# A hybrid decoder layer on one core: joint last tiles in three stages, and a final normalization that goes by thirds of the rows

## The reference

```python
h = rmsnorm(x, g_mix); z = h @ w_in            # 6656 columns: qa ka va ga (1024 each), qb 1024, kb 256, vb 256, gb 1024
oa = combine(dilated attention of 16 heads, windows/steps (128,1) (512,4) (2048,16))
ob = sliding window attention, 16 query heads, 4 key heads, 128 keys back, with sinks
h  = x + concat(oa * silu(ga), ob * silu(gb)) @ w_out
y  = h + (p @ w_ple) * sigmoid(rmsnorm(h, g_ple) @ w_pg)
return rmsnorm(y, g_final), and the new keys and values
```

## Time and profile before

| | |
|---|---|
| time, median of 3 runs | 2685.92 us (2680.72 to 2686.15) |
| the profiled execution's own time | 2688.74 us |
| its span, first to last instruction | 2686.9 us |
| TensorE busy | 2468.8 us (92%) |
| VectorE, ScalarE, POOL busy | 861.3, 610.3, 621.5 us |
| mean granted TensorE clock | 0.958 |
| mean DMA rate | 107 GB/s |

### The profile page before, as it was taken

How to read it: one execution, slowest core, us unless ns; L and a number is a source line. 1 busy time by engine, 2 the same in 40 slices (tenths; PEclk the granted TensorE clock), 3 DMA queues, 4 the chain that set the end, 5 groups by cost and what they waited for, 6 DMA issues and landing times.

```text
span 2686.9 us, 40432 instructions
## 1 busy us (share of the span) xinstructions
PE 2468.8 (92%) x16617; PEld 2298.9 (86%) x16617; DVE 861.3 (32%) x2136; ACT 610.3 (23%) x1458; POOL 621.5 (23%) x653
## 2 busy tenths in 40 slices
PE   4999999999999999999899887899999969999970
PEld 3998888888888898888788887799999859999970
DVE  7022332332332304445544223231101163323224
ACT  5022222222222213335454000120000131101013
POOL 2222222222222232222111321234333201111110
PEclk7999999999999999999999998899999979999995
DMA  4132222232322234434443442443323253232326
GB/s 170 57 117 93 87 91 91 91 97 85 96 90 83 70 99 133 136 112 131 143 121 116 130 142 76 135 145 95 89 75 90 78 184 96 73 96 74 94 70 235
DMA packets 301962, 287.95 MB, mean 107 GB/s; under 512 B 20865, under 2 KB 267449, under 8 KB 298425
## 3 DMA queue, kind: packets, MB, share of 16 engines
q1 hardware_dynamic: 278898, 241.11, 29.8%
q10 hardware_dynamic: 17856, 27.34, 3.0%
q0 software_dynamic: 5024, 16.92, 1.7%
HBM read 215.48 MB, written 69.81 MB: 106 GB/s over the span
## 4 chain that ended last, share of the span: by engine, by line
PE 83%; DVE 7%; DMA 6%; ACT 2%; issue 1%; POOL 1%; SPq 1%; POOLq 0%; DVEq 0%; ACTq 0%
PE psum L813 18%; PE psum L815 17%; PE psum L814 17%; PE psum L886 5%; PE psum L888 5%; PE psum L887 5%; PE psum L618 3%; PE psum L634 3%; PE psum L646 3%; DMA s_ring<-in_cache_a_v 1%; PE psum L837 1%; DMA out<-f_out 1%; PE psum L674 1%; DMA s_ring<-in_cache_a_k 1%; PE psum L689 1%
## 5 line engine op out<-in xcount | busy, mean ns | idle before, releaser
L813 PE MATMUL psum<-act_hi,w_hi 128*128 128x344 f32 x3264 | 1078.9, 331 | 14.1 <-DVE act_lo L1364 13.1
L815 PE MATMUL psum<-act_hi,w_lo 128*128 128x344 f32 x3264 | 1051.9, 322 | 0.0
L814 PE MATMUL psum<-act_lo,w_hi 128*128 128x344 f32 x3264 | 1051.5, 322 | 0.0
L813 PEld LDWEIGHTS psum<-act_hi,w_hi 128*128 128x128 f32 x3264 | 623.6, 191 | 25.7 <-issue 20.1
L814 PEld LDWEIGHTS psum<-act_lo,w_hi 128*128 128x128 f32 x3264 | 622.7, 191 | 0.0
L815 PEld LDWEIGHTS psum<-act_hi,w_lo 128*128 128x128 f32 x3264 | 622.1, 191 | 0.0
L575 POOL CAST w_hi<-w_raw 128x512 fp32r<-128x512 f32 x272 | 182.4, 671 | 1547.9 <-PE psum L815 1406.6
L577 POOL TENSOR_TENSOR w_lo<-w_raw,w_hi 128x512 fp32r<-128x512 f32 x272 | 366.5, 1348 | 21.8
L1162 DVE COPY prob_t<-psum 128x512 f32<-128x512 f32 (+2 forms) x96 | 53.5, 558 | 470.0 <-PE psum L646 470.0
L584 POOL DMA_DIRECT2D y_scratch<-y_nat x48 | 36.7, 764 | 425.1 <-ACT y_nat L1092 415.5
L886 PE MATMUL psum<-act_hi,u_even 128*128 128x344 f32 x384 | 125.5, 327 | 9.4 <-DVE u_even L1387 8.3
(11 more groups left out here) (198 smaller groups left out, 2742.1 us busy)
## 6 DMA issues: line engine op xcount, KB each, us to landing
w_raw<-in_w_in SPq DMA_DIRECT2D x208, 256.0 KB, 3.0
w_raw<-in_w_out SPq DMA_DIRECT2D x64, 256.0 KB, 2.8
u_raw<-in_w_pg SPq DMA_DIRECT2D x16, 1024.0 KB, 6.3
z_scratch<-stage ACTq DMA_DIRECT2D x72, 172.0 KB, 1.8
h_scratch<-h_row ACTq DMA_DIRECT2D x16, 516.0 KB, 3.3
h_stage<-h_scratch SPq DMA_DIRECT2D x16, 516.0 KB, 4.7
h_in<-h_scratch SPq DMA_DIRECT2D x48, 172.0 KB, 2.6
x_in<-in_x_prompt SPq DMA_DIRECT2D x8, 1024.0 KB, 5.1
```

Of the source, the lines that this page charges most:

```text
L813: pe.matmul(psum[:, bank, 0:T3], w_hi[:, slot, x, :], act_hi[:, k, rows], start=(k == 0), stop=False, skip_group_check=True)
L814: pe.matmul(psum[:, bank, 0:T3], w_hi[:, slot, x, :], act_lo[:, k, rows], start=False, stop=False, skip_group_check=True)
L815: return pe.matmul(psum[:, bank, 0:T3], w_lo[:, slot, x, :], act_hi[:, k, rows], start=False, stop=stop, skip_group_check=True)
```

## The change

The input projection's last two tiles (52 - 2 = 50 on, `ZPAIR` = unit 150) are made together, k outermost, with six banks; so are the last two output tiles (`HPAIR` = 14). While they are made, y tiles 0 to 13 (h tiles 0 to 13) are loaded back and split in the places of `act_hi` and `act_lo` that the joint tiles have used up (`x_used`, `yk_used`). The y tiles of the pair itself stay in SBUF (`y_last`). All 16 output tiles have k outermost. p is turned beside output tiles 1 to 9. Squares of h are summed in thirds. Gate tile 0 has k outermost, and the three mean matmuls stand behind its k = 11 and k = 14.

Gate weights go through the same groups, raw slots and ring as the others (4 groups of 4 k tiles and one of 2 per tile), loaded by SP and split by POOL; those of the last tile have their own space (`last_hi`, `last_lo`). Gate tiles 14 and 15 go third by third of the rows (`GATES`). The squares of y are summed from PSUM by ScalarE, piece by piece, and ScalarE issues the stores to `y_scratch`. When a third of both last tiles is done, its rows are loaded back into the parts of `act_hi` and `act_lo` that it frees (`f_rows`), the two last column tiles are put beside them from PSUM, and the rows are scaled by VectorE (or, for pieces 2, 4 and 5, by POOL) and stored.

In `events()` the sample sequences stand 88 places apart instead of 96, with other offsets, and mixer B's part is moved ahead, with its eight score transposes in one place (`sb` 1). g_ple is loaded at the start.

```diff
+GATES = [(n, t) for n in range(KT - 2) for t in range(3)] + [(n, t) for t in range(3) for n in (KT - 2, KT - 1)]
+GSPLIT = 3 * (KT - 2)
+ROW_PIECES = [(T3 * t + c0, n) for t in range(3) for c0, n in PIECES[t]]
...
+        first = 1448 + 88 * b
+        for i, at in enumerate((0, 1, 16, 22, 34, 72)):
             put(first + at, "sa_load", b, i)
-        for t, at in enumerate((8, 13, 24)):
+        for t, at in enumerate((8, 13, 26)):
             put(first + at, "sk", b, t)
...
+        for step, at in ((1, 42), (2, 58), (3, 70), (4, 83), (5, 87)):
             put(first + at, "sa", b, step)
-    put(2226, "sb_rows")
-    put(2240, "sb", 0)
+    put(2160, "sb_rows")
+    put(2174, "sb", 0)
     for b in range(NB):
-        put(2250 + 14 * b, "sb_seq", b)
-    put(2370, "sb", 1)
-    put(2400, "sb", 2)
-    put(2420, "sb", 3)
-    put(2440, "sb", 4)
+        put(2184 + 14 * b, "sb_seq", b)
+    put(2330, "sb", 1)
+    put(2350, "sb", 2)
+    put(2366, "sb", 3)
+    put(2382, "sb", 4)
...
+        last_hi, = at(B0 + 3072, ("last_hi", [P, KT + 2, P], F32R))
+        last_lo, = at(B0 + 16512, ("last_lo", [P, KT + 2, P], F32R))
+        squares, f_rms = at(B0 + 34400, ("squares", [P, 9, KT], F32), ("f_rms", [P, 5, 3], F32))
...
+        f_rows = [place(1, 0), place(1, P), place(0, 0), place(1, T3), place(1, T3 + P), place(0, T3), place(0, T3 + P), place(1, 0), place(1, P)]
+        gf_row = place(0, P)
...
+            sp.dma_start(gcol[:], a["g_ple"].rearrange("a (k p) -> p (a k)", p=P), allow_slow_non_contiguous=True).then_inc(sem("consts"), 16)
...
+            sp.wait_ge(sem("sb_done"), 1)
+            sp.wait_ge(sem("y_gated"), ZPAIR - GATE0)
+            for j in range(6):
+                i, t = divmod(ZPAIR - GATE0 + j, 3)
+                w = T3 if t < 2 else S - 2 * T3
+                sp.dma_start(o_last[:, j, 0:w], o_dram[i, :, T3 * t:T3 * t + w]).then_inc(sem("o_last_loaded"), 16)
+            for slot, count in stored(ZPAIR - 1):
                 sp.wait_ge(sem(f"stored{slot}"), 16 * count)
...
+            first = GROUP["in", NZ - 2, 0]
+            for k in range(HPAIR):
+                if k >= 3:
+                    sp.wait_ge(sem("y_split"), k - 2)
+                sp.dma_start(y_in[:, k % 3, :], yt_dram[k]).then_inc(sem(f"y_loaded{k % 3}"), 16)
+                if k % WG == 1 and k > WG:
+                    weights(first + 2 * (k // WG) + 5)
+                    weights(first + 2 * (k // WG) + 6)
             load_x_cols(0)
...
+            weights(first + 13)
+            weights(first + 14)
...
+            for n in range(KT - 2):
+                first = GROUP["gate", n, 0]
+                for t in range(2):
+                    load_h_in(3 * n + t)
                 if n:
...
-            sp.wait_ge(sem("u_produced"), 3 * KT)
+                    load_h_in(3 * n + 2)
+                for part in range(5 if n < KT - 3 else 10):
+                    weights(first + part + 7)
+                if n == 0:
+                    load_h_in(2)
+            def load_f(i):
+                r0, n = ROW_PIECES[i]
+                cols = (KT - 2) * P
+                sp.dma_start(f_rows[i][0:n, 0:KT - 2, :], y_dram[r0:r0 + n, 0:cols].rearrange("p (k c) -> p k c", c=P)).then_inc(sem(f"f_loaded{i}"), 16)
+            def store_f(i, count):
+                r0, n = ROW_PIECES[i]
+                sp.wait_ge(sem("f_scaled"), count)
+                m = min(n, S - r0)
+                sp.dma_start(yp[r0:r0 + m, :].rearrange("p (k c) -> p k c", c=P), f_rows[i][0:m]).then_inc(sem("out_stored0"), 16)
+                if m < n:
+                    sp.dma_start(ys.rearrange("p (k c) -> p k c", c=P), f_rows[i][m:n]).then_inc(sem("out_stored0"), 16)
+            for u in range(3):
+                load_h_in(GSPLIT + u)
             for par in range(2):
...
+                sp.wait_ge(sem(f"y_stored{par}"), 32 * (GSPLIT // 2))
+            sp.wait_ge(sem("u_produced"), GSPLIT + 2)
+            for i in range(3):
+                load_f(i)
+            sp.dma_start(gf_row, bcast_rows(a["g_final"].rearrange("(a d) -> a d", a=1), P).rearrange("p (k c) -> p k c", c=P)).then_inc(sem("gf_loaded"), 16)
+            load_h_in(GSPLIT + 3)
+            store_f(0, 1)
+            store_f(1, 2)
+            sp.wait_ge(sem("u_produced"), GSPLIT + 4)
+            for i in range(3, 7):
+                load_f(i)
+            sp.wait_ge(sem("out_stored0"), 32)
+            load_f(7)
+            load_f(8)
+            load_h_in(GSPLIT + 4)
+            load_h_in(GSPLIT + 5)
+            store_f(3, 3)
+            for i in range(6, 9):
+                store_f(i, i - 2)
+            sp.wait_ge(sem("out_stored0"), 16 * 7)
+            sp.wait_ge(sem("out_stored1"), 16 * 3)
...
+                last = what in ("gate", "ple") and i == KT - 1
                 pool.wait_ge(sem(f"w_loaded{g % 2}"), 16 * (g // 2 + 1))
...
+                if last:
+                    k += KT if what == "ple" else 0
+                    hi, lo = last_hi[:, k:k + n], last_lo[:, k:k + n]
+                    if k == 0:
+                        pool.wait_ge(sem("h_split"), KT)
+                        pool.wait_ge(sem("h_summed"), 3 * KT)
+                        for par in range(2):
...
+            pool.wait_ge(sem("gf_loaded"), 16)
+            for done, i in enumerate((2, 4, 5)):
+                r0, n = ROW_PIECES[i]
+                pool.wait_ge(sem(f"f_loaded{i}"), 16)
+                pool.wait_ge(sem("f_inverted"), i // 3 + 1)
+                pool.tensor_tensor(f_rows[i][0:n], f_rows[i][0:n], gf_row[0:n], ALU.mult).then_inc(sem("f_weighed"), 1)
+                pool.wait_ge(sem("f_weighed"), 2 * done + 1)
+                pool.tensor_scalar(f_rows[i][0:n], f_rows[i][0:n], f_rms[0:n, 1 + i // 3, i % 3:i % 3 + 1], None, ALU.mult).then_inc(sem("f_weighed"), 1)
+                pool.wait_ge(sem("f_weighed"), 2 * done + 2)
+                pool.dma_start(yp[r0:r0 + n, :].rearrange("p (k c) -> p k c", c=P), f_rows[i][0:n]).then_inc(sem("out_stored1"), 16)
...
+                elif e[0] == "sb" and e[1] == 1:
+                    pe.wait_ge(sem("bnew_scored"), 1)
+                    pe.wait_ge(sem("sa_ended"), 2 * NB)
+                    pe.transpose(psum[0:HEADS, 5, 0:NB], bnew[:], ident[0:NB, 0:NB]).then_inc(sem("bnew_rowed"), 1)
+                    pe.wait_ge(sem("sb_copied"), 3)
+                    pe.wait_ge(sem("sb_scored"), NB)
+                    for b in range(NB):
+                        mm = pe.transpose(psum[0:HEADS, 2 + b // 4, P * (b % 4):P * (b % 4 + 1)], bsc[:, b, :], ident[:])
+                    mm.then_inc(sem("sb_rowed"), 1)
...
+            pe.wait_ge(sem("bank_free"), ZPAIR)
+            pe.wait_ge(sem("sb_done"), 1)
+            for k in range(KT):
+                for i in range(2):
+                    group_wait("in", NZ - 2 + i, k)
+                    for t in range(3):
+                        mm = three(3 * i + t, "in", NZ - 2 + i, k, t, k == KT - 1)
+                        if k == KT - 1:
+                            mm.then_inc(sem("produced"), 1)
+                    if k < KT - 1 and i == 1:
+                        mm.then_inc(sem("x_used"), 1)
+                    elif k < KT - 1 and k % WG == WG - 1:
+                        mm.then_inc(sem("w_used"), 1)
...
+            pe.wait_ge(sem("h_bank_free"), 3 * HPAIR)
             for k in range(KT):
...
+                for i in range(2):
+                    group_wait("out", HPAIR + i, k)
+                    for t in range(3):
+                        mm = three(h_banks[i][t], "out", HPAIR + i, k, t, False)
+                    if i == 1:
+                        mm.then_inc(sem("yk_used"), 1)
+                    elif k % WG == WG - 1:
+                        mm.then_inc(sem("w_used"), 1)
+            residual(HPAIR)
+            residual(HPAIR + 1)
...
+            pe.wait_ge(sem("p_lo"), len(ROW_TILES))
+            for k in range(KT):
+                group_wait("gate", 0, k)
+                pe.wait_ge(sem("h_split"), k + 1)
                 for t in range(3):
...
+                    if k == 0 and t == 2:
+                        pe.wait_ge(sem("h_bank_free"), 3 * HPAIR + 1)
+                    mm = three(4 + t, "gate", 0, k, t, k == KT - 1)
+                if k % WG == WG - 1:
+                    mm.then_inc(sem("w_used"), 1)
+                if k == 11:
+                    pe.wait_ge(sem("h_summed"), 3 * KT)
+                    pe.wait_ge(sem("h_bank_free"), 3 * KT)
+                    mean_square(0)
+                    mean_square(1)
+                elif k == 14:
+                    pe.wait_ge(sem("h_eps"), 1)
+                    mean_square(2)
+            for t in range(3):
+                embedding(t)
+            for u in range(3, 3 * KT):
+                n, t = GATES[u]
+                pe.wait_ge(sem("p_read"), u - 2)
+                for k in range(KT):
+                    if t == 0:
+                        group_wait("gate", n, k)
```

(33 more changed lines are left out.)

551 lines of the change are left out of this document (288 added, 263 removed).

## The result

| | before | changed | ratio, 95% interval |
|---|---|---|---|
| median | 2683.3 us (4 runs) | 2596.4 us (2594.6 to 2596.9, 4 runs) | 0.9676 [0.9659, 0.9692] |
| span of the profiled execution | 2686.9 | 2595.1 | |
| mean granted TensorE clock | 0.958 | 0.972 | |
| TensorE, VectorE, ScalarE, POOL busy | 2468.8, 861.3, 610.3, 621.5 | 2451.2, 831.8, 635.0, 711.8 | |

The account below looks back on a forecast made before the run. TensorE is busy throughout the long product stretches; only its stops and the low clock after them can be won. Terms +1.5 - 65 - 14 + 3 - 34 - 43 = -151.5 from 2688.7, less 2.8, gave 2535 us; range 2505 to 2585.

Parts of the forecast that it names:

- The mechanisms of the joint tiles: Last two input and last two output tiles: products hide loading and splitting of earlier tiles; -14 and -34 us.
- A single stop: Sign in the gate: TensorE stops once, about 5 us, after the first gate tile, ended by t_gate or p_read on VectorE.
- One of the prediction's own signs of being wrong: The prediction is wrong if TensorE waits for w_lo or y splits, or if sample waits stay above 25 us.
- slower: Rival, gate: the ring of weight groups cannot feed it; a group must take 7.6 us to eat the gain; 3%.
- p's transposes: Output projection: the nine transposes of p move here from the gap, about 3 us at full clock, +3.
- Against this steps 4 and 5 are only 4 places apart: Input projection, mixer A: the closeness of two steps set against its denser plan, within a term of -65 us.
- POOL's rows cost by its rows 4 x 1.29 + 4 x 0.61 = 7.6 us each: Tail: time POOL needs for each row piece it handles, 7.6 us.
- they land at Z + 45: Tail: last two units' h_in loads land 45 us after Z, the end of both last tiles' first third.
- the tail's term: Tail after the last gate product: 39 us instead of 82, so -43 us; bounds -22 and -50.
- The waits of the sample work stay: Rival, input projection: each sample may keep a 2 to 4 us wait; only 33 of 65 us come; 2567 us; 17%.
- the tail keeps most of its length: Rival, tail: h_in loads queue behind slow stores and POOL's rows follow; tail 62 us, time 2558 us; 17%.
- the sample term: Input projection, sample work: named TensorE waits and the low clock they cause mostly go; -65 us, bounds -30 and -76.

## Why the prediction was too low

**Right.** The mechanisms of the joint tiles, both times: no stream starved, and the losses left are 5.9 us (forecast 3) and 9.7 us (forecast 9). A single stop followed the first gate tile, ended by VectorE's reading of the embedding bank (L1644, whose semaphore is p_read, as forecast), 6.2 us long for 4.6. POOL's ring fed the gate: no wait for w_lo there, 0.2 us for last_lo. One of the prediction's own signs of being wrong did come, TensorE waiting for w_lo, but for 2.3 us, once, in the input projection. So the rival "slower" never came near its point. p's transposes cost 1.5 for 3. Mixer B's batch gave its 26 us alone.

**The step that failed in the sample work** is "Against this steps 4 and 5 are only 4 places apart", as the only thing set against mixer A's denser plan. The sum put a wait for keys at nothing. VectorE waits 39.4 us for them instead of 5.8, and what is queued behind it on VectorE, mixer B's maxima, holds TensorE. The first scoring stayed 8 places behind its load, but VectorE now comes to it sooner than SP's list lets the keys land. The margin of the ring shrank too, from 12 places (5.7 us) between step 4 and the next sequence's first place to 5 (2.4 us), but by the timelines it held back at most one load of seven. I had counted the waits that would go and looked at each semaphore's own margin, but not at when SP comes to a load, nor at who stands behind VectorE when it waits. Mixer A's share, some 30 of the 65 us, came out as zero where its plan was put alone into the kernel before, and came where the keys were moved in the changed one. Of the 41.7 us measured 26 are the batch, if its gain is the same here as alone, and about 5 the softmax's wait; the other 10 I can only place, in smaller waits and low clock, not prove.

**The steps that failed in the tail** are two, in the order of what they cost.
- "POOL's rows cost by its rows 4 x 1.29 + 4 x 0.61 = 7.6 us each": they take 4.50 + 5.44 to 7.36 = 10 to 12 us, a size that no row of before had. The exclusion was priced at the end only, 4 us; it also hit the first scalings (12.51 us instead of 4.7), hence unit 45 (5.7 us of TensorE) and SP's list, and the last root's small operations (9.6 us). Without POOL's part: -23.3.
- "they land at Z + 45": they landed at Z + 63. The mechanism was right (queued behind stores and six loads, VectorE stands at this add), two sizes were not. The stores could go out only at Z + 24.3 and Z + 30.0, instead of from Z + 16.7 on, since the gain row landed later and the two scalings were slow. From the second to the landing were 33.0 us: the forecast took 299 GB/s from a 2 us window of weight loads, and 27 us of row pieces of the same size ran at 219; SP was held for 24.1 of the 33.0 us in issuing the six row loads. With the loads moved: -20.3.

The two overlap; together they are 35.5 us, the 35 that the tail's term missed.

By the Trainium skill, "SBUF — State Buffer", section "Who interferes with whom", a VectorE instruction with two SBUF inputs and a GpSimd instruction that reads SBUF exclude each other for a whole instruction, and operations such as tensor_scalar can take the shared ports too. The trace agrees that both are slowed: 12.51 us for two scalings beside POOL's pair and 4.62 without it, and 4.80 us for a tensor_scalar over 3 columns. It does not bear out that every pair excludes each other wholly: the second of the two scalings ends 0.4 us behind POOL's tensor_scalar, and the four instructions take 12.5 us where one after the other they would take 4.6 + 4.6 + 5.4 = 14.6; later an add over 344 columns (0.52 us alone) takes 2.42 us within another such tensor_scalar and ends over 1 us ahead of it. What failed most was the list of places where the rule was applied.

**The range** failed in one more way. "The waits of the sample work stay" (2567) and "the tail keeps most of its length" (2558) were set as alternatives, 17% each. They are independent, and both came in part: the sample term lost 23 us where the first had 32, by a wait for keys that it did not name, and the h_in loads and POOL's rows made the tail long as the second had it. Both in full, 32 + 23 us above the forecast, are 2590, already above the range's end of 2585, and the tail was 12 us longer than the second had it (73.8 for 62).

## What to carry to other kernels

When a hand-written plan is made denser, read for every load in the timeline when its slot comes free, when the in-order queue issues it, when it lands and when its reader is ready; here most slots were free well before the issue, and the reader had become ready sooner. For every wait on an in-order engine, ask which other engine's work stands behind it; a list of TensorE's present waits shows only what can be won, not what appears. When a stage is overlapped by cutting rows into thirds, price the traffic at the rate of the pieces it is cut into, put the small load that the last products need ahead of the bulk, and compare the work on one engine with the work split over two that slow each other (here one was 23 us faster); and if two rivals don't exclude each other, the range has to hold both at once.

## What was not expected of the hardware

- How long SP is held by issuing a DMA depends on the pieces and on what is under way. Row loads in parts of 512 bytes took 0.37 and 0.86 us in the changed kernel when they were the first of a series, and 2.3 to 6.5 us in the series of six; two of the last stores took 5.85 and 3.16 us, the two first ones 0.64 and 0.55. Eight loads of whole rows in a series take 3.74 us together. A small load behind such a series in program order waits for all of it: 24.1 us here.
- The DMA engines are busy 0.92 to 0.98 of the time at 219 to 289 GB/s with parts of 512 bytes in SBUF, and 0.95 at 371 GB/s with 8 KB rows: the busy share does not tell the rate.
- A VectorE instruction over three columns can take 5.55 us instead of 0.16: it starts while POOL issues a store, 1 us ahead of POOL's tensor_tensor over 2048 columns, and ends with it.
